# A streaming encoder step on one core: Query's streamed weight pieces split around its resident half, and two of tile 0's V groups moved from tile 2's recurrence to tile 1's top-k

## The chip, the core and the metric

The kernel runs on one core of a Trainium2 chip. The metric is device time of one execution in microseconds (us); the kernel before takes 2175.14 us (median of 3 runs, 2174.68 to 2177.02). Everything is computed in fp32.

## What is computed

One layer over a prompt (16 meta tokens and 512 tokens) and a sample of 64 tokens: RMS norm, one combined projection, forgetting attention and an HGRN2 recurrence, output projection and residual; then a retrieval of single-neuron experts (PEER). The last part is what matters here:

```python
def peer_ffn(x, w_query, sub_keys, expert_u, expert_v):     # cut
    q = (xb @ w_query).reshape(T, 8, 2, 128)                # 1024 -> 2048 columns
    s = jnp.einsum('thcd,hcnd->thcn', q, sub_keys)          # scores against 2 x 8 x 128 keys
    sa, ia = lax.top_k(s[:, :, 0], 16); sb, ib = lax.top_k(s[:, :, 1], 16)
    ...                                                     # top 16 of the 256 sums: eidx, gate
    act = jax.nn.gelu(jnp.einsum('thkd,td->thk', expert_u[eidx], xb), approximate=False)
    return jnp.einsum('thk,thkd->td', gate * act, expert_v[eidx])
```

Each token chooses 128 of 16384 rows of `expert_u` and as many of `expert_v`, each row 4 KB.

## The kernel before

The tokens are five tiles: tile 0 (sample and meta tokens) and tiles 1 to 4 of 128 prompt tokens. For each tile t the engines run attention (8 heads), the recurrence (stages named levels, masks, gram0 to gram3), norm, output projection, the second norm ("rows"), Query, and top-k. Each engine has its program in one fixed order and meets the others by semaphores alone.

**The expert rows.** GpSimd (POOL) issues 576 gathers for U (L592) and 576 for V (L598), each one row per partition, 512 KB. They land in a ring of 17 slots; a gather waits until the slot's last user is done. A U row group is multiplied by VectorE (DVE, L1387, a "dot"), a V row group by TensorE (PE, L1044) with a diagonal that ScalarE (ACT) makes from the gates (L820). Four V gathers are a quad, also called a group here; a quad is 16 matmul instructions. The gathers and their uses for tile t-1 are laid out among the stages of tile t by tables: `DOT_PLACES` for U; for V, `NEXT_PLACES` puts quads of tile t-1 at "top" of tile t itself, beside its top-k, and `LEFT_PLACES` puts what is left into tile t+1. For tile 0, which has 64 V values (16 quads) where the others have 128, the constants are `FIRST_NEXT` and `FIRST_LEFT_PLACES`. In the program's list the U gathers of tile t start only when the top-k of tile t has written its indices (`chosen`, after L1633).

**The streamed weights.** `w_out` (8 pieces) and the second half of `peer_w_query` (8 pieces) pass through five slots of `lev`, 512 KB each, and are numbered 0 to 15 in each tile. SyncE (SP) loads piece c when piece c-5 has been used:

```python
                for c in range(DC + WO_RING, 2 * DC):               # 13, 14, 15
                    sp.wait_ge(wo_used, 2 * DC * t + c - WO_RING + 1)
                    load_w_out(c)
```

Pieces 0 to 4 are asked for when the recurrence's outputs are done, 5 to 12 during the output projection, 13 to 15 as pieces 8, 9 and 10 are used. PE uses a piece in `streamed` (L1233, four matmul instructions in the profile: two halves of 512 columns, and the profile shows each matmul as two). The first half of `peer_w_query` lies resident in `arena` (L1254). Query is: wait for the turned rows, 16 resident matmuls into PSUM tensor PB, then pieces 8 to 15 into PA, then the turning of both results (L1266, which wait for ACT's copies L932 and L935), then the keys (L1275), which release DVE's top-k (L1580 on).

Of the kernel before, what the change touches and what calls it, by code (L numbers as in the profile page):

```python
# [30 lines left out]
DC = D // P  # L31
# [39 lines left out]
PARTS = TILES - 2  # L71
WO_RING = 5

LEVELS = [64, 32, 16, 8, 4, 2, 1]
NL = len(LEVELS)
NEG = -1e30
# [9 lines left out]
    ("levels", 3), ("masks", 3), ("gram1", 2), ("gram2", 2)]  # L86
NEXT_PLACES = [("top", 13)]

FIRST_NEXT = 10
FIRST_LEFT_PLACES = [("levels", 2), ("masks", 2), ("gram1", 1), ("gram2", 1)]  # L90


LATER = TILES - 1
# [21 lines left out]
def build(nc, x_prompt, x_sample, cache_kt, cache_v, cache_logf, state_hgrn, meta_tokens, w_in,  # L115
# [4 lines left out]
    with ExitStack() as ctx:  # L120
# [3 lines left out]
        def sem(name):  # L124
            return ctx.enter_context(nc.semaphore(name))

        PA, PB, PC, PD = [ctx.enter_context(nc.psum_tensor(n, [P, D], F32)) for n in ("PA", "PB", "PC", "PD")]
# [99 lines left out]
        gram_done, at_ready, ho_done, ho_evac, st_done, st_new, mix_ready = (sem(n) for n in (  # L227
            "gram_done", "at_ready", "ho_done", "ho_evac", "st_done", "st_new", "mix_ready"))
# [52 lines left out]
        def first_level(t):  # L281

            return 0 if t else 1
# [72 lines left out]
        for t in range(1, TILES):  # L356
# [6 lines left out]
            if t == 1:  # L363
                n_next = FIRST_NEXT * QUAD
            if t > 1:
                first = values_before(t - 2) + (n_next if t > 2 else FIRST_NEXT * QUAD)
                places = LEFT_PLACES if t > 2 else FIRST_LEFT_PLACES
# [8 lines left out]
            for place, quads in NEXT_PLACES:  # L376
                values_at[t, place] = range(taken, min(end, taken + (FIRST_NEXT if t == 1 else quads) * QUAD))
                taken = values_at[t, place].stop
# [582 lines left out]
        def _(pe):  # L961
# [89 lines left out]
            for t in range(TILES):  # L1051
# [175 lines left out]
                def streamed(c, out, n):  # L1227

                    slot = c % WO_RING
                    per_tile = len(range(slot, 2 * DC, WO_RING))  # L1230
                    pe.wait_ge(wo_in[slot], 16 * (per_tile * t + c // WO_RING + 1))
                    for half in range(2):
                        last = pe.matmul(out[:, half * 512:(half + 1) * 512], rows_t[:, c % DC * P:c % DC * P + n],  # L1233
                                         w_out_sb[:, slot, half * 512:(half + 1) * 512],
                                         start=(c % DC == 0), stop=(c % DC == DC - 1))
                    last.then_inc(wo_used, 1)
                    return last
# [11 lines left out]
                    pe.wait_ge(wq_in, 16 * DC)  # L1249
                nq = P if t else N_SAMPLE  # L1250
                pe.wait_ge(x1_ready, t + 1)
                for half in range(2):
                    for c in range(DC):
                        last = pe.matmul(PB[0:nq, half * 512:half * 512 + 512], rows_t[:, c * P:c * P + nq],  # L1254
                                         w_query_sb[:, c, half * 512:half * 512 + 512], start=(c == 0), stop=(c == DC - 1))
                last.then_inc(pq_done, 1)
                weighted_quads(PD, t, "pq0")
                pe.wait_ge(ho_evac, t + 1)
                for c in range(DC, 2 * DC):
                    streamed(c, PA[0:nq, :], nq)  # L1260
                weighted_quads(PD, t, "pq1")
                for n, psum in enumerate((PB, PA)):
# [26 lines left out]
        def _(eng):  # L1289
# [116 lines left out]
            for t in range(TILES):  # L1406
# [75 lines left out]
                for l in range(first_level(t), NL):  # L1482
                    m = LEVELS[l]
                    out, src = halves(lev[:, l * HW:(l + 1) * HW], HW // (2 * m), m), halves(sums, HW // (2 * m), m)
# [15 lines left out]
                for l in range(first_level(t), NL):  # L1500
                    m = LEVELS[l]
                    both = halves(lev[:, l * HW:(l + 1) * HW], HW // (2 * m), m)
# [161 lines left out]
def constant_columns():  # L1664
# [6 lines left out]
            np.where(t <= s, 0.0, NEG), np.broadcast_to(np.arange(TOPK)[None, :], (P, TOPK))]  # L1671
    for m in LEVELS:
        cols.append((s // (2 * m) == t // (2 * m)) & (s // m % 2 == 0) & (t // m % 2 == 1))
# [47 lines left out]
```

## Time and profile before

| | us |
|---|---|
| median of 3 runs | 2175.14 |
| profiled execution: its own time | 2177.34 |
| profiled execution: span of the trace | 2175.1 |
| busy PE / DVE / POOL / ACT | 1220.8 / 1263.5 / 1165.9 / 373.4 |
| moved by DMA, mean rate | 722.04 MB, 332 GB/s |

Busy time counts no waits and no issuing of DMAs by SP. A row of the chain of waits is a piece of the work that ended last: its start, its length, what it was. A row of a timeline is a run of like instructions on one engine; the bracket at its end is the idle time before it and what ended it.

### The profile page before, as it was taken

What the parts mean: (1) busy time and instruction counts of PE and PEld (TensorE: products, weight loads), DVE (VectorE), ACT (ScalarE), POOL (GpSimd) and SP (SyncE); (2) the same over time, 40 slices, a digit from 0 to 9 for tenths busy, and PEclk for the clock granted to TensorE, in tenths of its full rate; (3) what the DMA queues carried; (4) which work ended last, traced back from release to release, by engine and by line L of the source; (5) the groups of instructions that cost most, each with busy time, mean ns of one, the idle gap of its engine ahead of it and who ended that gap; (6) DMA issues with size and microseconds to landing.
All of it is one profiled execution on the core that took longest, in us unless ns stands there. A gap on an engine that the chain in (4) does not pass through costs nothing.

```text
span 2175.1 us, 15704 instructions
## 1 busy us (share of the span) xinstructions
PE 1220.8 (56%) x4932; PEld 538.3 (25%) x4932; DVE 1263.5 (58%) x2795; ACT 373.4 (17%) x1034; POOL 1165.9 (54%) x1197
## 2 busy tenths in 40 slices
PE   5898778474881365843445574445567322223564
PEld 2544343243331222311222231222332000000110
DVE  3344430877388976786564677576477566654001
ACT  1221211011030121221121121112103100002211
POOL 3012110242446774577767457776745767777673
PEclk9798879686995577976668696665778566555766
DMA  9211174485987999999999999999999999999997
GB/s 338 95 59 46 71 276 131 158 303 170 345 328 308 410 409 410 389 372 410 409 369 408 411 386 372 409 409 373 409 411 358 378 409 409 409 409 409 411 409 280
DMA packets 204307, 722.04 MB, mean 332 GB/s; under 512 B 23249, under 2 KB 25537, under 8 KB 203073
## 3 DMA queue, kind: packets, MB, share of 16 engines
q0 software_dynamic: 171168, 624.01, 73.6%
q1 hardware_dynamic: 33056, 97.03, 12.1%
q8 instruction: 40, 0.66, 0.1%
q14 instruction: 43, 0.34, 0.0%
HBM read 704.71 MB, written 15.70 MB: 331 GB/s over the span
## 4 chain that ended last, share of the span: by engine, by line
DMA 28%; PE 26%; DVE 16%; POOL 11%; issue 5%; ACT 4%; DVEq 0%; POOLq 0%; ACTq 0%
DMA arena<-peer_expert_v,idx_v 18%; POOL arena L598 7%; DMA arena<-peer_expert_u,idx_all 7%; PE PD L1044 6%; DVE arena L1387 4%; POOL arena L592 4%; PE PB L1254 4%; PE PD L966 3%; PE PB L1233 3%; DMA lev<-w_out 2%; PE PA L1233 2%; PE PA L1184 2%; DMA lev<-peer_w_query 2%; PE PB L1121 1%; PE PA L1044 1%
## 5 line engine op out<-in xcount | busy, mean ns | idle before, releaser
L592 POOL DMA_INDIRECT arena<-peer_expert_u,idx_all x576 | 543.7, 944 | 462.4 <-DVE arena L1387 185.1
L1387 DVE SCALAR_TENSOR_TENSOR arena<-arena,PC 128x1024 f32<-128x1024 f32 x576 | 677.6, 1217 | 159.6 <-DMA arena<-peer_expert_u,idx_all 152.6
L598 POOL DMA_INDIRECT arena<-peer_expert_v,idx_v x576 | 565.4, 982 | 259.7 <-issue 142.7
L1044 PE MATMUL PD<-arena,diag_v 128*32 128x512 f32 x1792 | 362.0, 883 | 516.4 <-DMA arena<-peer_expert_v,idx_v 491.2
L1044 PEld LDWEIGHTS PD<-arena,diag_v 128*32 128x32 f32 x1792 | 80.4, 141 | 755.7 <-issue 755.4
L820 ACT ACTIVATE diag_v<-consts,gate_all 128x32 f32<-128x32 f32 x576 | 137.5, 310 | 570.6 <-PE PD L1044 445.7
L966 PE MATMUL PD<-arena 128*128 128x512 f32 x384 | 178.4, 621 | 0.0
L1044 PE MATMUL PA<-arena,diag_v 128*32 128x512 f32 x512 | 96.4, 891 | 70.9 <-DMA arena<-peer_expert_v,idx_v 70.9
L1233 PE MATMUL PB<-lev,rows_t 128*128 128x512 f32 x160 | 87.9, 709 | 22.9 <-DMA lev<-w_out 17.3
L966 PEld LDWEIGHTS PD<-arena 128*128 128x128 f32 x384 | 75.1, 200 | 88.1 <-issue 87.5
L1452 DVE TENSOR_TENSOR PA<-PA,consts 128x128 f32<-128x128 f32 (+4 forms) x56 | 14.0, 250 | 140.4 <-PE PA L1102 140.1
L1121 PE MATMUL PB<-v_pr,w 128*128 128x64 f32 (+1 forms) x224 | 51.4, 374 | 59.4 <-ACT w L879 59.4
L1254 PE MATMUL PB<-arena,rows_t 128*128 128x512 f32 (+1 forms) x160 | 79.8, 663 | 5.6 <-ACT rows_t L929 5.6
L860 ACT ACTIVATE w<-PA,small 64x576 f32<-64x576 f32 (+5 forms) x48 | 25.2, 526 | 306.0 <-DVE small L1455 299.6
L1647 DVE TENSOR_TENSOR lev<-lev,PD 128x1024 f32<-128x1024 f32 x1 | 1.2, 1221 | 130.1 <-PE PA L1044 130.1
L1233 PE MATMUL PA<-lev,rows_t 128*128 128x512 f32 (+1 forms) x160 | 72.6, 600 | 4.8 <-DMA lev<-peer_w_query 4.6
L1522 DVE TENSOR_TENSOR w<-PA,level_masks 128x1024 f32<-128x1024 f32 (+1 forms) x18 | 21.8, 1209 | 80.9 <-PE PA L1185 80.9
L1121 PEld LDWEIGHTS PB<-v_pr,w 128*128 128x128 f32 (+1 forms) x224 | 43.0, 265 | 93.8 <-ACT w L879 64.3
L1102 PE MATMUL PA<-k_pr,qa 128*16 128x16 f32 (+5 forms) x96 | 38.1, 497 | 33.2 <-issue 33.2
L1044 PEld LDWEIGHTS PA<-arena,diag_v 128*32 128x32 f32 x512 | 20.0, 139 | 147.4 <-issue 147.4
L651 POOL DMA_DIRECT2D arena<-w_in x4 | 3.6, 899 | 94.6 <-PE PD L966 94.6
L1233 PEld LDWEIGHTS PB<-lev,rows_t 128*128 128x128 f32 x160 | 35.7, 231 | 73.0 <-issue 40.4
(271 smaller groups left out, 1509.7 us busy)
## 6 DMA issues: line engine op xcount, KB each, us to landing
lev<-w_out SPq DMA_DIRECT2D x40, 512.0 KB, 11.1
lev<-peer_w_query SPq DMA_DIRECT2D x40, 512.0 KB, 8.5
arena<-w_in SPq DMA_DIRECT2D x8, 2048.0 KB, 14.0
arena<-peer_expert_u,idx_all POOLq DMA_INDIRECT x576, 9.8
arena<-peer_expert_v,idx_v POOLq DMA_INDIRECT x576, 10.9
arena<-w_in POOLq DMA_DIRECT2D x4, 2048.0 KB, 8.6
act<-staged SPq DMA_DIRECT2D x4, 1796.0 KB, 8.7
staged<-arena POOLq DMA_DIRECT2D x5, 1024.0 KB, 5.2
```

Source lines behind the costliest of these rows:

```text
L592: pool.indirect_dma_start(slot, None, peer_expert_u[0], bass.IndirectOffsetOnAxis(ap=idx_all[:, k:k + 1], axis=0)).then_inc(arrived, 16)
L598: pool.indirect_dma_start(slot, None, peer_expert_v[0], bass.IndirectOffsetOnAxis(ap=idx_v[:, k:k + 1], axis=0)).then_inc(arrived, 16)
L820: return eng.activation(diag_v[:, at * STRIP:(at + 1) * STRIP], consts[:, C_FOLD:C_FOLD + STRIP], ACT.Copy, scale=gate_all[:, k:k + 1])
L860: eng.activation(w1[0:m, D * (a % 2):D * (a % 2) + n], score_psum(a, n)[0:m, :], ACT.Exp, bias=negmax[0:m, h:h + 1], accum_out=psums[0:m, ...
L966: last = pe.matmul(out, x[:, c * P:(c + 1) * P], weights[:, c, :], start=(c == 0), stop=(c == DC - 1))
L1044: ins = pe.matmul(psum[c * STRIP:(c + 1) * STRIP, half * 512:(half + 1) * 512], diag_v[:, at * STRIP:(at + 1) * STRIP], ring[slot_of[v_pla ...
L1102: last = pe.matmul(score_psum(a, n)[0:m, k0:k1], qa[:, h * P + q0:h * P + q0 + m], keys[:, h, k0:k1], start=True, stop=True)
L1121: last = pe.matmul(attended(t)[0:m, h * HD:(h + 1) * HD], w2[0:k, at:at + m], value_rows(t, q0, i, k, h // (HEADS // KV_HEADS)), start=(i ...
L1184: pe.matmul(psum[:, l * P:(l + 1) * P], both, both, start=True, stop=True)
L1233: last = pe.matmul(out[:, half * 512:(half + 1) * 512], rows_t[:, c % DC * P:c % DC * P + n], w_out_sb[:, slot, half * 512:(half + 1) * 51 ...
L1254: last = pe.matmul(PB[0:nq, half * 512:half * 512 + 512], rows_t[:, c * P:c * P + nq], w_query_sb[:, c, half * 512:half * 512 + 512], star ...
L1387: eng.scalar_tensor_tensor(out=slot, in0=slot, scalar=1.0, in1=h2_dots[:, :], op0=ALU.mult, op1=ALU.mult, accum_out=out).then_inc(free, 1)
```

## The change

The number of pieces that the ring cannot yet hold when Query starts, 3, becomes `QUERY_FIRST`. PE now uses pieces 8, 9 and 10 ahead of the resident half and pieces 11 to 15 behind it. `FIRST_NEXT` goes from 10 to 12, and the places for tile 0's remaining quads in tile 2 hold 4 instead of 6.

```diff
+QUERY_FIRST = DC - WO_RING
...
-FIRST_NEXT = 10
-FIRST_LEFT_PLACES = [("levels", 2), ("masks", 2), ("gram1", 1), ("gram2", 1)]
+FIRST_NEXT = 12
+FIRST_LEFT_PLACES = [("levels", 2), ("masks", 1), ("gram1", 1)]
...
                 pe.wait_ge(x1_ready, t + 1)
+
+                pe.wait_ge(ho_evac, t + 1)
+                for c in range(DC, DC + QUERY_FIRST):
+                    streamed(c, PA[0:nq, :], nq)
                 for half in range(2):
                     for c in range(DC):
                         last = pe.matmul(PB[0:nq, half * 512:half * 512 + 512], rows_t[:, c * P:c * P + nq],
                                          w_query_sb[:, c, half * 512:half * 512 + 512], start=(c == 0), stop=(c == DC - 1))
                 last.then_inc(pq_done, 1)
                 weighted_quads(PD, t, "pq0")
-                pe.wait_ge(ho_evac, t + 1)
-                for c in range(DC, 2 * DC):
+                for c in range(DC + QUERY_FIRST, 2 * DC):
                     streamed(c, PA[0:nq, :], nq)
```

No instruction is added or dropped on any engine. Two places, in the order in which the engines run them (line numbers of the changed file are 2 to 5 higher; a row counts matmuls, of which the profile shows two instructions each):

PE, Query of tile 1, from the turning of the rows to the keys, before and then changed.

```order
L1244 MATMUL PA<-consts,rows 128x128 x8
L1254 MATMUL PB<-arena,rows_t 128x512 x16
L1233 MATMUL PA<-lev,rows_t 128x512 x16
L1266 MATMUL PB<-consts,w 128x128 x8
L1266 MATMUL PA<-consts,w 128x128 x8
```

```order
L1246 MATMUL PA<-consts,rows 128x128 x8
L1235 MATMUL PA<-lev,rows_t 128x512 x6
L1260 MATMUL PB<-arena,rows_t 128x512 x16
L1235 MATMUL PA<-lev,rows_t 128x512 x10
L1271 MATMUL PB<-consts,w 128x128 x8
```

Six streamed matmuls (three pieces) moved ahead of the sixteen resident ones; the Querys of the other four tiles change in the same way.

POOL, from tile 0's U gathers (64) on: tile 0's V beside tile 1's top-k, then tile 2's attention and recurrence with tile 1's U, before and then changed.

```order
L592 DMA arena<-peer_expert_u,idx_all 128x1024 x64
L598 DMA arena<-peer_expert_v,idx_v 128x1024 x40
L592 DMA arena<-peer_expert_u,idx_all 128x1024 x76
L598 DMA arena<-peer_expert_v,idx_v 128x1024 x4
L592 DMA arena<-peer_expert_u,idx_all 128x1024 x2
L598 DMA arena<-peer_expert_v,idx_v 128x1024 x4
L592 DMA arena<-peer_expert_u,idx_all 128x1024 x3
L598 DMA arena<-peer_expert_v,idx_v 128x1024 x4
L592 DMA arena<-peer_expert_u,idx_all 128x1024 x2
L598 DMA arena<-peer_expert_v,idx_v 128x1024 x4
L592 DMA arena<-peer_expert_u,idx_all 128x1024 x4
L598 DMA arena<-peer_expert_v,idx_v 128x1024 x4
```

```order
L594 DMA arena<-peer_expert_u,idx_all 128x1024 x64
L600 DMA arena<-peer_expert_v,idx_v 128x1024 x48
L594 DMA arena<-peer_expert_u,idx_all 128x1024 x76
L600 DMA arena<-peer_expert_v,idx_v 128x1024 x4
L594 DMA arena<-peer_expert_u,idx_all 128x1024 x2
L600 DMA arena<-peer_expert_v,idx_v 128x1024 x4
L594 DMA arena<-peer_expert_u,idx_all 128x1024 x5
L600 DMA arena<-peer_expert_v,idx_v 128x1024 x4
L594 DMA arena<-peer_expert_u,idx_all 128x1024 x4
L600 DMA arena<-peer_expert_v,idx_v 128x1024 x4
L594 DMA arena<-peer_expert_u,idx_all 128x1024 x41
```

Eight V gathers moved from the recurrence of tile 2 to the burst beside tile 1's top-k; what stays in the recurrence is two quads at "levels", one at "masks" and one at "gram1". The second quad of "masks" and the one of "gram2" are gone there, and their 32 matmul instructions on PE with them.

## Rows read from the trace of the kernel before

**Rows 1.** The page: rate of DMA in 40 slices; the chain's shares by engine.

```profile
GB/s 338 95 59 46 71 276 131 158 303 170 345 328 308 410 409 410 389 372 410 409 369 408 411 386 372 409 409 373 409 411 358 378 409 409 409 409 409 411 409 280
...
DMA 28%; PE 26%; DVE 16%; POOL 11%; issue 5%; ACT 4%; DVEq 0%; POOLq 0%; ACTq 0%
```

**Rows 2.** The chain of waits in Query of tile 1: start, length, what.

```profile
589.26 8.55 DMA lev<-peer_w_query
```

**Rows 3.** Timeline of PE, Query of tile 1: start, length, line, count, idle before.

```profile
583.92 10.81 PE L1233 MATMUL PA<-lev,rows_t 128*128 128x512 f32 x24
595.30 1.98 PE L1233 MATMUL PA<-lev,rows_t 128*128 128x512 f32 x4 [0.58 <-DMA lev<-peer_w_query]
597.86 1.98 PE L1233 MATMUL PA<-lev,rows_t 128*128 128x512 f32 x4 [0.57 <-DMA lev<-peer_w_query]
599.68 1.04 PE L1266 MATMUL PB<-consts,w 128*128 128x128 f32 x8
```

**Rows 4.** The same timeline, Query of tile 0.

```profile
364.24 13.90 PE L1233 MATMUL PA<-lev,rows_t 128*64 128x512 f32 x32
378.06 0.71 PE L1266 MATMUL PB<-consts,w 64*128 64x64 f32 x8
```

**Rows 5.** The page's groups: Query's streamed matmuls, all tiles; busy, then idle before.

```profile
L1233 PE MATMUL PA<-lev,rows_t 128*128 128x512 f32 (+1 forms) x160 | 72.6, 600 | 4.8 <-DMA lev<-peer_w_query 4.6
```

**Rows 6.** Timeline of SP, output projection of tile 2: pieces 8 to 12 asked for.

```profile
845.57 13.95 SPq L528 DMA_DIRECT2D lev<-peer_w_query  x5
```

**Rows 7.** Timeline of POOL beside tile 1's top-k and at tile 2's start.

```profile
612.73 0.94 POOL L598 DMA_INDIRECT arena<-peer_expert_v,idx_v  x1 [13.82 <-PE PD L1044]
...
641.30 0.94 POOL L598 DMA_INDIRECT arena<-peer_expert_v,idx_v  x1 [0.31 <-PE PD L1044]
662.25 0.94 POOL L592 DMA_INDIRECT arena<-peer_expert_u,idx_all  x1 [20.01 <-DVE idx_all L1633]
```

**Rows 8.** Timeline of PE, end of tile 1's top-k and start of tile 2.

```profile
647.74 3.63 PE L1044 MATMUL PD<-arena,diag_v 128*32 128x512 f32 x16 [1.41 <-DMA arena<-peer_expert_v,idx_v]
...
664.03 2.15 PE L1102 MATMUL PA<-k_pr,qa 128*128 128x272 f32 x4 [11.23 <-issue]
```

**Rows 9.** The chain of waits, recurrence of tile 2.

```profile
785.43 9.68 DMA arena<-peer_expert_v,idx_v
```

**Rows 10.** Timeline of PE, recurrence of tile 2: both quads of "masks", then gram1.

```profile
788.25 6.19 PE L1044 MATMUL PD<-arena,diag_v 128*32 128x512 f32 x16 [1.62 <-ACT diag_v L820]
795.36 3.63 PE L1044 MATMUL PD<-arena,diag_v 128*32 128x512 f32 x16 [0.92 <-DMA arena<-peer_expert_v,idx_v]
...
804.29 3.14 PE L1184 MATMUL PA<-lev 128*128 128x128 f32 x14 [3.32 <-DVE w L1524]
```

**Rows 11.** Timeline of PE, recurrence of tile 1 (no V quads there): gram3.

```profile
522.19 1.83 PE L1184 MATMUL PA<-lev 128*128 128x128 f32 x14 [2.37 <-DVE w L1524]
```

**Rows 12.** Stretches: busy of PE, PEld, DVE, ACT, POOL; PE clock; DMA share; GB/s.

```profile
804.20:807.50 3.30, 3.21 (x17) 3.24 (x18) 2.34 (x4) 0.00 (x0) 2.49 (x3) 0.56 1.02 408
...
848.00:867.00 19.00, 8.31 (x18) 3.91 (x19) 5.81 (x12) 1.69 (x3) 0.54 (x1) 0.77 1.03 410
```

**Rows 13.** Timeline of PE, output projections of tile 2 and (last row) of tile 1.

```profile
835.64 11.61 PE L1233 MATMUL PB<-lev,rows_t 128*128 128x512 f32 x20 [1.11 <-ACT rows_t L925]
852.05 6.25 PE L1233 MATMUL PB<-lev,rows_t 128*128 128x512 f32 x10 [4.80 <-DMA lev<-w_out]
...
556.96 1.98 PE L1233 MATMUL PB<-lev,rows_t 128*128 128x512 f32 x4 [0.44 <-DMA lev<-w_out]
```

**Rows 14.** DMA queues of 848 to 862 us, output projection of tile 2: packets, MB, share.

```profile
q1 hardware_dynamic: 788, 2.88, 51.5%
q0 software_dynamic: 780, 2.85, 51.2%
```

**Rows 15.** The eight U gathers asked for at 867 to 877 us, tile 2.

```profile
DMA to landing us min/median/max: 11.9/12.0/12.1
```

**Rows 16.** Timeline of DVE, tile 2: last use of the dots of tile 1.

```profile
905.13 0.29 DVE L1404 TENSOR_TENSOR dots_all<-dots_all,gate_all 128x128 f32<-128x128 f32 x1 [10.88 <-ACT dots_all L840]
```

## The prediction, before the changed kernel was run

> **What bounds the kernel now.** I read the page first. Its 40 slices are 54.4 us each: DMA runs at 46 to 345 GB/s in the first 13 and then, from 707 us on, at 408 to 411 GB/s in most, with dips [rows 1]. The chain of waits is mixed: DMA 28%, PE 26%, DVE 16%, POOL 11% [rows 1]. So neither a busy share nor the mean rate says what an edit is worth; each stage has to be asked which wait ends last. A microsecond taken from the PE/DVE chain of a tile reaches the end if the gathers restart from that chain afterwards, which they do once per tile: the ring is full, POOL stands (13.82 us in tile 1) and the first V quads on PE, behind Query, set it going again [rows 7]. The last 450 us are one stream of gathers at the DMA limit, and start so much earlier.
>
> About 0.2% (4.3 us) is what a measurement of this kernel can tell from no change.
>
> **First part: Query's order.** In tile 1 the streamed matmuls start at 583.92 and the next work on PE at 599.68: 15.76 us for 32 instructions. In tile 0, where no wait is shown, the same 32 take 378.06 - 364.24 = 13.82 us [rows 3, 4]. The difference, 1.94 us, stands around the two shown gaps of 0.58 and 0.57 us before pieces 14 and 15, and a smaller one before 13 [rows 3]: those pieces are asked for only when 8, 9 and 10 have been used, and take 8.55 us on the chain [rows 2]. Over all tiles the gaps are 4.6 us [rows 5], four times the 1.15 of tile 1, so tiles 1 to 4 behave alike and tile 0 has nothing to win.
>
> Now 8, 9 and 10 go first. They were asked for long before: in tile 2 SP issued 8 to 12 between 845.57 and 859.52 [rows 6], all during the output projection, and between that and Query lie the sum, the second norm and the turning of the rows, some 10 us, in which PE uses no piece. Pieces 13 to 15 are then asked for some 15 us earlier, and between their request and their use lie the resident half and two pieces, over 17 us against 8.55. So the gaps go, nothing takes their place, and each of four tiles gives 1.94 us; the shown gaps alone, 1.15, are the lower price. ACT's copy of PB comes 5.2 us later than now, but 5 pieces (8.6 us) still run behind it and hide its 1 us. **4 x 1.94 = 7.8 us, bounds 4.6 and 7.8.**
>
> What is moved along: three 512 KB loads per tile now fall into the 10 us in which POOL restarts its U gathers. Those eight gathers land in 12.0 us [rows 15]; 1.5 MB more at 410 GB/s adds 3.7 us. DVE, which needs them, has 10.88 us to spare before ACT's gelu lets it go on [rows 16]. I take nothing for it.
>
> **Second part: two quads, beside tile 1's top-k.** POOL issues the last of 40 V gathers there at 641.30, at 1.25 us each, and then stands 20.01 us until the top-k has written its indices [rows 7]. Eight more are 10.0 us: they end 10 us before the U gathers of tile 2 may start, and cost POOL nothing. On PE the last quad now starts 647.74, 6.4 us after its last gather was issued; two more, 5 us apart, end at about 661.4, then the turning of tile 2's q and k (1.5 us), done near 663. PE now begins the scores at 664.03 after standing 11.23 us [rows 8]. So the cover is thin but there; if the landings took 10 us instead of 6.4, tile 2 would start up to 3 us late.
>
> What it wins is in tile 2, in two places.
>
> *Recurrence.* The chain waits there for V gathers: 9.68 us of landing before the second quad of "masks" [rows 9]. PE runs the two quads of "masks" at 788.25 and 795.36, ending at 799.0 [rows 10]. With one quad, its last gather is issued after five U and four V instead of five U and eight V: some 5 us earlier, so it lands about 790. If it ran in 3.63 us, PE would be done at 794; the first of the two took 6.19 us [rows 10], the slower kind that follows a wait, so I take 796.2. That wins 2.8 us. At "gram2" a quad of 3.63 us goes, but behind a gram without a quad PE stands 2.37 to 3.32 us for DVE's mask and sum [rows 10, 11], say 2.8, so 0.8 us is all there is. Against it stands PE's clock. After a gap of 3.32 us the 14 matmuls of gram1 took 3.14 us, at a mean granted clock of 0.56 (mostly the 1.2 GHz level); after 2.37 us in tile 1 they took 1.83 [rows 10, 11, 12]. The new gap before gram3 is some 2.8 us, between the two, so gram3 may lose 1.3 us or nothing. I take 0.5 won at gram2 and **3.3 us for the recurrence**, bounds 2 and 5.8. The Trainium skill ("TensorE: Matmul & The Clock Gate", the section "Why this matters for your kernels") says that idle gaps between bursts of matmuls send the array back to half rate, which speaks against taking a quad out. [...]
>
> *Output projection.* PE does five pieces in 11.61 us, stands 4.80 us for the sixth, and needs over 6.25 us for the last three, where twelve instructions at the 0.43 us of tile 0's Query would take 5.2: 4.8 + 1.9 = 6.7 us of waits [rows 4, 13]. It stands although POOL has been stopped: from 848 to 867 us POOL is busy 0.54 us and DMA is at 410 GB/s [rows 12]. The gathers issued before are still being served, and share the engines in halves with SP's loads: 2.85 and 2.88 MB [rows 14]. In tile 1, with no V gathers in the recurrence, the last piece waited 0.44 us [rows 13]. Take eight gathers (10.0 us of DMA) out ahead of this stage and let the chain come 3.3 us earlier, and the backlog is 6.7 us shorter: SP's loads have the engines to themselves while the ring is full. So between 0 and 6.7 us of these waits go. I take **4.5 us**, nearer to the upper end, since tile 1's row shows what a short backlog does. The two places together, 7.8 us, stay below the 10.0 us of DMA work that was moved, which is the bound of this part. The Trainium skill ("DMA: Bandwidth & Descriptors", "Queues, rings and completion order") says that each DMA engine goes round the queues that have work, which is what the halves look like. By that rule SP's loads go twice as fast from the moment at which the gathers' queue is empty, and the stage would win the whole 6.7.
>
> **Sum.** 7.8 + 3.3 + 4.5 = 15.6 us. Against the profiled execution's own time, 2177.3 (span 2175.1), that is 2161.7. The median of the runs is 2.2 us below that execution, so in terms of medians I forecast 2175.1 - 15.6, rounded: **2160 us**.
>
> **The rivals.**
>
> *A. The backlog does not shorten in time.* The twelve gathers that the "out" dots set going come in any case, right at the start of the projection, and alone can fill the queue (6.3 MB, 15 us at 410 GB/s). Then the output projection keeps its waits: 7.8 + 3.3 = 11.1 us, 2164. For it: the halves of [rows 14] are still there up to 14 us after POOL's last issue. Against it: tile 1's row.
>
> *B. The second part gives nothing.* PE's clock falls in the gaps that the quads leave (1.3 us in each of two grams), tile 2 starts a little late, the projection keeps its waits: 7.8 us, 2167.
>
> *C. The wait only changes its place.* Pieces 8 to 10 are late at the head of Query, or 11 and 12 behind it, and B holds as well: 2172 to 2175. Against it: the ten microseconds between SP's last issue and PE's first use.
>
> *D. Slower: the loads pulled forward hit the U gathers of "rows".* DVE's last dots, and so gelu, the V gates and POOL's restart, come late in tiles 1 to 4. It decides from the point where the landing of these gathers grows by more than the 10.88 us of slack [rows 16], from 12 to 23 us; to cost 20 us, enough to turn the forecast over, it must be 28. The added 1.5 MB is worth 3.7. The result would be near 2182.
>
> **How the numbers follow.** Forecast (2155 to 2162) 0.60, A 0.22, B 0.10, C 0.05, D 0.03. The likeliest is 2160. The range reaches down to the case that both parts pay their bound (7.8 + 10.0 with 1 or 2 us of luck with the clock, 2155) and up to B (2167) with a microsecond for the measurement: 2155 to 2168. All of the forecast, A and B is faster by more than 4.3 us: 0.92; C is within 0.2%: 0.05; D is slower: 0.03.
>
> **What would show it.** In the changed profile: no wait for `peer_w_query` before L1235 in any tile, and Query's 64 matmul instructions some 1.9 us shorter in tiles 1 to 4, unchanged in tile 0; POOL's idle time before tile 2's first U gather near 10 us instead of 20; 48 V gathers before it; PE's gap before tile 2's first scores near 1 us; tile 2's gram3 over 3 us earlier after its indices than now; the 4.80 us wait in tile 2's projection gone or under 2; and POOL's long wait before the "rows" gathers (L594) shorter by the projection's gain. Wrong would be: the landings of those eight U gathers above 20 us, DVE idle before L1406 near zero, tile 2's first dots late, or a gain in tile 2 that is given back as a longer wait of POOL in the top-k of tile 2 or 3.

## The result and the profile after

| | before | changed |
|---|---|---|
| median, us (5 runs each) | 2175.42 | 2164.09 |
| lowest and highest | 2174.68, 2183.06 | 2162.69, 2167.72 |
| profiled execution: its own time | 2177.34 | 2164.09 |
| profiled execution: span of the trace | 2175.1 | 2161.9 |
| busy PE / DVE / POOL / ACT | 1220.8 / 1263.5 / 1165.9 / 373.4 | 1217.1 / 1261.7 / 1169.8 / 373.4 |

The ratio of the runs is 0.9942 [0.9925, 0.9959]: 0.6% faster, 11.3 us by the medians and 13.2 us between the two profiled executions. Forecast were 2160 us and a gain of 15.6. A second set of the same kernel (below) gives 0.9939 [0.9927, 0.9952].

The page of the changed kernel: DMA rate in 40 slices, the chain's shares by engine, and the two groups of streamed matmuls (busy and mean, then idle before them).

```profile
GB/s 338 97 59 40 78 264 146 146 316 148 346 376 336 409 409 409 386 374 409 410 372 410 411 394 375 410 409 362 409 411 379 373 410 409 409 410 409 411 409 281
...
PE 27%; DMA 25%; DVE 13%; POOL 13%; issue 6%; ACT 4%; DVEq 0%; POOLq 0%; ACTq 0%
...
L1235 PE MATMUL PB<-lev,rows_t 128*128 128x512 f32 x160 | 85.1, 691 | 20.2 <-DMA lev<-w_out 14.7
...
L1235 PE MATMUL PA<-lev,rows_t 128*128 128x512 f32 (+1 forms) x160 | 81.4, 667 | 5.6 <-ACT rows_t L931 5.6
```

The 4.6 us of waiting for `peer_w_query` [rows 5] are gone; the 5.6 us in their place are the wait for the turned rows, which stood before the resident half until now (1.11 us in each tile). The DMA rate and the chain's mix hardly changed [rows 1].

**Query.** PE's timeline, Query of tile 1 (start, length, line, count, idle before):

```profile
569.39 7.84 PE L1235 MATMUL PA<-lev,rows_t 128*128 128x512 f32 x12 [1.11 <-ACT rows_t L931]
577.07 13.90 PE L1260 MATMUL PB<-arena,rows_t 128*128 128x512 f32 x32
590.81 8.75 PE L1235 MATMUL PA<-lev,rows_t 128*128 128x512 f32 x20
599.39 1.04 PE L1271 MATMUL PB<-consts,w 128*128 128x128 f32 x8
```

Nothing waits for a piece, where pieces 14 and 15 waited 0.58 and 0.57 us and their four instructions took 1.98 each [rows 3]; the last twenty now take 8.75 us. The stage from the first turning of the second norm's rows to the turning of the results takes, in tiles 1 to 4:

| us | tile 1 | 2 | 3 | 4 | sum |
|---|---|---|---|---|---|
| before | 34.13 | 34.21 | 34.85 | 34.63 | 137.8 |
| changed | 33.08 | 32.33 | 32.35 | 32.64 | 130.4 |

That is 7.4 us for the 7.8 of the sum; tile 0 kept its length (33.30, 33.53). Tile 1 won only 1.05: its first twelve instructions took 7.84 us, where twelve take 5.2 at the rate of the last twenty.

**The two quads.** POOL's timeline beside tile 1's top-k, and PE's at the end of it:

```profile
612.55 0.95 POOL L600 DMA_INDIRECT arena<-peer_expert_v,idx_v  x1 [12.66 <-PE PD L1046]
...
643.41 0.94 POOL L600 DMA_INDIRECT arena<-peer_expert_v,idx_v  x1 [0.30 <-issue]
644.66 2.48 POOL L600 DMA_INDIRECT arena<-peer_expert_v,idx_v  x1 [0.30 <-issue]
647.45 2.02 POOL L600 DMA_INDIRECT arena<-peer_expert_v,idx_v  x1 [0.30 <-issue]
...
652.27 2.14 POOL L600 DMA_INDIRECT arena<-peer_expert_v,idx_v  x1 [0.30 <-issue]
654.72 2.02 POOL L600 DMA_INDIRECT arena<-peer_expert_v,idx_v  x1 [0.30 <-issue]
662.08 0.94 POOL L594 DMA_INDIRECT arena<-peer_expert_u,idx_all  x1 [5.34 <-DVE idx_all L1638]
```

```profile
661.13 6.26 PE L1046 MATMUL PD<-arena,diag_v 128*32 128x512 f32 x16 [3.83 <-DMA arena<-peer_expert_v,idx_v]
667.32 1.06 PE L1063 MATMUL PA<-consts,act 128*64 128x128 f32 x8
```

The eight moved gathers are not eight times 1.25 us: four of them took 2.0 to 2.5. POOL waits 5.34 us for the indices, not 10, and tile 2's q and k are turned at 667.32, not 661.4 (651.29 before). The U gathers still start as before, 662.08 against 662.25 [rows 7].

**Tile 2.** Recurrence and output projection on PE:

```profile
789.99 4.98 PE L1046 MATMUL PD<-arena,diag_v 128*32 128x512 f32 x16 [3.33 <-DMA arena<-peer_expert_v,idx_v]
...
800.27 3.33 PE L1186 MATMUL PA<-lev 128*128 128x128 f32 x14 [3.31 <-DVE w L1529]
...
814.42 1.83 PE L1186 MATMUL PA<-lev 128*128 128x128 f32 x14 [2.78 <-DVE w L1529]
...
833.25 12.66 PE L1235 MATMUL PB<-lev,rows_t 128*128 128x512 f32 x24 [1.11 <-ACT rows_t L927]
846.47 1.98 PE L1235 MATMUL PB<-lev,rows_t 128*128 128x512 f32 x4 [0.56 <-DMA lev<-w_out]
849.36 1.98 PE L1235 MATMUL PB<-lev,rows_t 128*128 128x512 f32 x4 [0.90 <-DMA lev<-w_out]
```

The chain of waits there still runs through one V gather, before the quad that stayed at "masks":

```profile
780.09 9.65 DMA arena<-peer_expert_v,idx_v
```

The quad started at 789.99, where the forecast had its last landing ("about 790"), and PE is done with it at 794.90, 4.0 us earlier than with two quads. Some of that is lost at once. The clock in the stretches of gram1 and of gram3 (columns as in [rows 12]), and the quad of gram1, changed and then before:

```profile
800.20:804.80 4.60, 4.53 (x20) 4.34 (x20) 3.06 (x5) 0.00 (x0) 3.42 (x4) 0.50 1.03 408
814.40:816.50 2.10, 2.08 (x18) 2.09 (x19) 2.10 (x3) 0.00 (x0) 1.49 (x3) 1.00 1.02 406
...
804.80 4.41 PE L1046 MATMUL PD<-arena,diag_v 128*32 128x512 f32 x16
...
808.03 3.63 PE L1044 MATMUL PD<-arena,diag_v 128*32 128x512 f32 x16
```

After the gap of 3.31 us the whole of gram1 ran at a granted clock of 0.50, the 1.2 GHz level, and the quad behind it took 4.41 us instead of 3.63; after the gap of 2.78 us gram3 ran at 1.00. When the quad of gram1 is done (809.14 against 811.59), 2.5 of the 4.0 us are left.

The wait of 4.80 us in the projection [rows 13] is now 0.56 and 0.90. In tile 1's projection before, which the forecast took as the measure of a short backlog, two more pieces waited ahead of the one in [rows 13]:

```profile
551.97 1.98 PE L1233 MATMUL PB<-lev,rows_t 128*128 128x512 f32 x4 [0.50 <-DMA lev<-w_out]
554.53 1.98 PE L1233 MATMUL PB<-lev,rows_t 128*128 128x512 f32 x4 [0.58 <-DMA lev<-w_out]
```

From the first U gather to the turning of the mixed rows tile 2 takes 168.09 us (170.31 before), and from there to the turning of the second norm's rows 27.78 (33.21 before). What the two DMA queues moved at the start of the projection, before and then changed, and near its end, changed (packets, MB, share):

```profile
q0 software_dynamic: 229, 0.83, 52.4%
q1 hardware_dynamic: 228, 0.81, 50.5%
...
q1 hardware_dynamic: 248, 1.37, 86.9%
q0 software_dynamic: 60, 0.25, 15.5%
...
q1 hardware_dynamic: 221, 0.84, 52.4%
q0 software_dynamic: 222, 0.80, 50.3%
```

The first two pairs are 833 to 837 us, the third 849 to 853. The gathers' queue (q0) was all but empty when the changed projection began, so SP's loads (q1) had the engines nearly to themselves there. That lasted some 5 us, from 831 to 836: the gathers that POOL issued from 831.52 on then brought the halves back.

### The profile page after: what moved, and what is told of

It reads as the page before. It is cut to its first block, busy times and chain, and to the rows that moved or that the text cites. A ratio compares the mean times of both kernels' runs of the same rounds, so it can differ in the third digit from the quotient of the medians.

```text
span 2161.9 us, 15704 instructions
## 1 busy us (share of the span) xinstructions
PE 1217.1 (56%) x4932; PEld 542.4 (25%) x4932; DVE 1261.7 (58%) x2795; ACT 373.4 (17%) x1034; POOL 1169.8 (54%) x1197
## 4 chain that ended last, share of the span: by engine, by line
PE 27%; DMA 25%; DVE 13%; POOL 13%; issue 6%; ACT 4%; DVEq 0%; POOLq 0%; ACTq 0%
DMA arena<-peer_expert_v,idx_v 16%; POOL arena L600 9%; DMA arena<-peer_expert_u,idx_all 7%; PE PD L1046 7%; DVE arena L1392 5%; POOL arena L594 5%; PE PA L1235 4%; PE PD L968 3%; PE PB L1260 3%; PE PB L1235 3%; DMA lev<-w_out 2%; PE PB L1123 1%; PE PA L1186 1%; PE PA L1046 1%; DVE w L1529 1%
## 5 line engine op out<-in xcount | busy, mean ns | idle before, releaser
L1046 PE MATMUL PD<-arena,diag_v 128*32 128x512 f32 x1792 | 367.8, 896 | 516.1 <-DMA arena<-peer_expert_v,idx_v 491.0
L1046 PE MATMUL PA<-arena,diag_v 128*32 128x512 f32 x512 | 87.9, 821 | 79.3 <-DMA arena<-peer_expert_v,idx_v 79.3
L1235 PE MATMUL PA<-lev,rows_t 128*128 128x512 f32 (+1 forms) x160 | 81.4, 667 | 5.6 <-ACT rows_t L931 5.6
L1260 PE MATMUL PB<-arena,rows_t 128*128 128x512 f32 (+1 forms) x160 | 69.5, 592 | 0.0
L1186 PE MATMUL PA<-lev 128*128 128x128 f32 x248 | 42.6, 339 | 20.8 <-DVE w L1529 20.8
## 6 DMA issues: line engine op xcount, KB each, us to landing
arena<-peer_expert_v,idx_v POOLq DMA_INDIRECT x576, 10.5
```

Of the source, the lines that this page charges most:

```text
L1046: ins = pe.matmul(psum[c * STRIP:(c + 1) * STRIP, half * 512:(half + 1) * 512], diag_v[:, at * STRIP:(at + 1) * STRIP], ring[slot_of[v_pla ...
L1186: pe.matmul(psum[:, l * P:(l + 1) * P], both, both, start=True, stop=True)
```

## The experiments

Each is the changed kernel with the edit shown. The kernel before ran beside each of the four sets (median 2178.3, 2177.8, 2177.0 and 2177.6 us), and ratios are to it.

**1. Query's order alone.**

```diff
-FIRST_NEXT = 12
-FIRST_LEFT_PLACES = [("levels", 2), ("masks", 1), ("gram1", 1)]
+FIRST_NEXT = 10
+FIRST_LEFT_PLACES = [("levels", 2), ("masks", 2), ("gram1", 1), ("gram2", 1)]
```

> Query's pieces split as in the change (3 ahead of the resident half), tile 0's V quads left as before (10 beside tile 1's top-k). Theory (two independent gains: gaps before pieces 13 to 15; backlog of gathers in tile 2): Query is 1 to 2.3 us shorter in each of tiles 1 to 4, 4 to 8 us in all, so 2167 to 2171; the second tile's output projection keeps its waits (33.2 us from the turning of the mixed rows to the turning of the normed rows, the sixth piece waits over 4 us). Rival 1 (the pieces' new place also relieved the projection): that stretch of tile 2 falls to 28 us here too, and the time is near 2164. Rival 2 (the gain of the change was all the quads'): 2174 to 2176.

Measured: 2168.99 us, ratio 0.9956 [0.9942, 0.9971]. Query takes 33.66, 32.25, 32.30 and 32.71 us in tiles 1 to 4, 6.9 less than before; tile 2's projection keeps its 33.20. Tile 1's Query, 0.5 us shorter, stayed under the 1 us expected for each tile.

**2. The quads alone.**

```diff
-QUERY_FIRST = DC - WO_RING
+QUERY_FIRST = 0
```

> Tile 0's V quads as in the change (12 beside tile 1's top-k), Query in its old order. Theory: tile 2's recurrence is 2 to 3 us shorter and its projection stretch 28 instead of 33.2 us; Query of tiles 1 to 4 has its gaps of 0.57 us before pieces 14 and 15 again; 5 to 8 us in all, so 2167 to 2170. Rival 1 (the projection was relieved by Query's new order): 33 us in that stretch, 2172 to 2175. Rival 2 (both parts remove the same wait, so they do not add): 2164 to 2166 alone.

Measured: 2171.08 us, 0.9962 [0.9948, 0.9976], 1 us above what was expected. Tile 2's projection takes 27.96 us, the stretch from the first U gather to the mixed rows 167.57. In tile 1's Query pieces 13 to 15 wait again, 0.56 to 0.58 us each, and Query takes 139.9 us in tiles 1 to 4 (137.8 before). So both gains of tile 2, in its recurrence and in its projection, come from the quads and need nothing of Query's. The two parts, 0.44% and 0.38%, make 0.82% against 0.6% for both; with intervals of 0.15% each that may be less than the sum of both, but it isn't shown.

**3. Fourteen groups instead of twelve.**

```diff
-FIRST_NEXT = 12
-FIRST_LEFT_PLACES = [("levels", 2), ("masks", 1), ("gram1", 1)]
+FIRST_NEXT = 14
+FIRST_LEFT_PLACES = [("levels", 2)]
```

> The change, with 14 quads beside tile 1's top-k and 2 (levels) in tile 2: eight more gathers moved. Theory (the cover beside the top-k is used up on PE at 12): POOL's U gathers of tile 2 start at about 662 or up to 2 us later, PE ends the last quad at 672 or later and turns tile 2's q and k after it, so DVE's first dots of tile 2 come 5 to 10 us late; against that the recurrence gains at most 5 us and the projection at most the 1.5 us of waits that are left: 2162 to 2168, no gain. Rival (only the DMA work ahead of tile 2's projection counts): another 5 to 10 us faster, 2154 to 2159.

Measured: 2164.83 us, 0.9936 [0.9922, 0.9951], the time of the changed kernel. POOL, PE and DVE at the start of tile 2:

```profile
665.43 0.95 POOL L600 DMA_INDIRECT arena<-peer_expert_v,idx_v  x1 [0.30 <-issue]
666.69 0.95 POOL L594 DMA_INDIRECT arena<-peer_expert_u,idx_all  x1 [0.30 <-issue]
```

```profile
675.72 1.06 PE L1063 MATMUL PA<-consts,act 128*64 128x128 f32 x8
```

```profile
678.46 1.20 DVE L1392 SCALAR_TENSOR_TENSOR arena<-arena,PC 128x1024 f32<-128x1024 f32 x1
```

The cover of the burst is used up: the U gathers start 4.6 us late, q and k are turned 8.4 us later than in the changed kernel, and DVE's first dot follows them. Yet the mixed rows of tile 2 are turned at 826.78, 3.4 us before the changed kernel's 830.17: with two fewer quads in it, the tile made up for all of it. By tile 3 the lead is 0.9 us. This kernel changes two things at once, the late start and the number of quads. The kernels with the same four quads in tile 2 as the changed one separate them. In four executions (the changed kernel twice, experiment 4, the second set of experiment 6) DVE's first dot comes 7.2 to 8.1 us after the first U gather, and from that gather to the mixed rows tile 2 takes 167.9 to 168.8 us. In the seven others (2, the first set of 6, and 7 to 11 below) it comes 4.3 to 4.5 us after it, and the stretch is 167.5 to 169.2 us. The 667.32 of the changed kernel therefore cost nothing that can be seen.

**4. Six dots at the output projection instead of twelve**, so that fewer gathers are set going at its start:

```diff
-    ("out", 12), ("rows", 25)]
+    ("out", 6), ("rows", 31)]
```

> The change, with 6 of tiles 1 to 4's dots at the place 'out' (beside the output projection) instead of 12, and 31 instead of 25 at 'rows' (beside Query). Theory (SP's weight loads share the DMA engines with the gathers that the 'out' dots set going): the waits for w_out in tiles 3 and 4 (5 to 7 us each) fall by 3 to 6 us each, tile 2's rest by 1: 6 to 12 us faster than the change, 2152 to 2158; DVE's slack before the gelu falls from 9 us to about 2. Rival 1 (DMA is the limit over the whole tile, so that what the projection wins is lost when the gathers restart): 2162 to 2166, with POOL's wait beside the top-k shorter and PE's first V quads waiting for DMA. Rival 2 (DVE becomes late): slower than 2166, DVE not idle before the gelu.

Measured: 2162.83 us, 0.9926 [0.9912, 0.9941], where 2152 to 2158 was expected. The projections of tiles 3 and 4 stayed at 33.7 and 32.7 us, so what I wanted to relieve there was not relieved. Tile 1's went from 27.84 to 26.51, and its Query to 32.17. The interval overlaps the changed kernel's.

**5. The changed kernel again.**

> The changed kernel once more, unaltered, to see how far a stage of one execution can be trusted. Expected: within 0.1% of its first measurement (ratio 0.993 to 0.996). If the 2 us that went missing between the turning of Query's rows in tile 2 and the mixed rows of tile 3, and again in the next tile, belong to the change, that stretch stays near 306 us in both places; if they are the scatter of one execution, it comes out 1 us or more lower in at least one of them.

Measured: 2164.02 us. Between Query of tile 2 and the mixed rows of tile 3 the first execution took 305.9 us, this one 302.7; one tile later 306.1 and 307.9. So single stages of this length scatter by 2 to 3 us from one execution to the next. Query (131.0 us in tiles 1 to 4), tile 2's projection (27.82) and its stretch before (168.21) repeat within 0.6; tile 3's projection does not (33.76 and 35.27).

**6. One piece ahead instead of three**, run in two sets:

```diff
-QUERY_FIRST = DC - WO_RING
+QUERY_FIRST = 1
```

> The changed kernel with one piece ahead of the resident half instead of three. Theory (the wait was the ring's: piece c is asked for when c-5 has been used, lands some 8.6 us later, and only the resident half in between can cover it): piece 13 is covered, pieces 14 and 15 are not; the wait stands before piece 14 with at least 1 us in tiles 1 to 4, Query gives back 1 to 1.9 us per tile, and the time is 4 to 7 us above the changed kernel's, near that of the kernel with the quads alone (2171). Rival (any piece used ahead of the resident half gives the load enough head start, or Query gained by its order on PE and not by the loads): Query keeps its 32.3 to 33.1 us per tile, and the time is the changed kernel's.

> The kernel with one piece ahead of the resident half once more, since its first profiled execution showed Query 5.0 us longer over tiles 1 to 4 than the changed kernel's, and its five times did not show it. If the loss is real for the end, the median of this set lies 2 us or more above that of the changed kernel (2164), and both sets together too. If one piece ahead is worth as much as three, it comes to 2164 again; then the profile shows Query at 33.4 to 34.3 us again, and the time is given back in another stage.

Measured: 2164.07 us, 0.9938 [0.9925, 0.995], and 2165.56, 0.9945 [0.9932, 0.9959]. PE's timeline in Query of tile 1, first set:

```profile
587.31 10.77 PE L1235 MATMUL PA<-lev,rows_t 128*128 128x512 f32 x24
598.65 1.98 PE L1235 MATMUL PA<-lev,rows_t 128*128 128x512 f32 x4 [0.57 <-DMA lev<-peer_w_query]
```

The wait did come back, but before piece 15: piece 14 stands inside the row of 24, which takes 10.77 us instead of some 10.5. Query takes 135.4 and 136.4 us in tiles 1 to 4, 4.4 to 6.0 more than with three pieces ahead. The spans of the profiled executions follow (2165.5 and 2167.6 against 2161.9 and 2162.8), but they were the slowest of their sets both times; over all runs the mean is 2165.5 for one piece (10 runs) and 2164.7 for three (11 runs), with a scatter of 2.1 in each. So it is shown that the edit removes the ring's wait. The 4 to 7 us that were expected at the end did not come, and whether the end gets those 5 us at all stays open.

**7 and 8. What makes a gather slow.** In the changed kernel's trace the slow gathers beside the top-k end 0.8 us after a long DVE instruction does. DVE's timeline beside them:

```profile
644.04 2.29 DVE L1626 TENSOR_TENSOR w<-lev,consts 128x2048 f32<-128x2048 f32 x1
646.37 2.29 DVE L1628 TENSOR_TENSOR w<-w,lev 128x2048 f32<-128x2048 f32 x1
648.70 2.29 DVE L1629 TENSOR_REDUCE lev<-w 128x128 f32<-128x2048 f32 x1
```

The gather of 644.66 ends at 647.14, that of 647.45 at 649.47; L1626 and L1628 end at 646.33 and 648.66. In the whole trace 20 gathers start while a `tensor_tensor` of 128x2048 runs, and all 20 take 1.92 to 2.49 us; the 12 that are already under way when one starts take 0.94 to 0.95. A gather that runs beside the reduction (649.78) takes 0.94, and 0.94 is also the length beside the dots, whose second input is in PSUM. Two kernels test it. In the first the three kinds of long `tensor_tensor` (L1605, L1626, L1628) go head by head (the edit is shown for one kind, the others are alike):

```diff
-                    link(eng.tensor_tensor(same, same, idx_h[:, :, c, :].unsqueeze(2).to_broadcast(shape), ALU.mult))
+                    for h in range(ph):
+                        last = eng.tensor_tensor(same[:, h:h + 1], same[:, h:h + 1],
+                                                 idx_h[:, h:h + 1, c, :].unsqueeze(2).to_broadcast(one), ALU.mult)
+                    link(last)
```

> The changed kernel with the three kinds of long tensor_tensor in top-k (the sums of candidates, the comparison with the counting row, the product with the indices; each 128x2048 with both inputs in SBUF) done as eight of 128x256. Theory (a gather whose descriptors POOL writes while such an instruction runs has to wait until it ends): no gather over 1.5 us beside the top-k any more, where the changed kernel has 26 of 1.3 us and more; POOL issues the last V gather of tile 1's burst 4 to 5 us earlier, tile 2's q and k are turned 3 us earlier or more. DVE pays 35 more instructions per tile, 2 to 3 us, and that lies on the chain of every top-k, so the time is 5 to 12 us above the changed kernel's. Rival (what slows a gather is DVE writing 128x2048 of data, or the queue's own memory traffic, not the length of one instruction): the gathers stay at 2 us.

Measured: 2162.9 us, 0.9932 [0.992, 0.9945]. POOL at the same place, and DVE:

```profile
645.83 0.95 POOL L600 DMA_INDIRECT arena<-peer_expert_v,idx_v  x1 [0.30 <-issue]
647.08 1.04 POOL L600 DMA_INDIRECT arena<-peer_expert_v,idx_v  x1 [0.31 <-PE PD L1046]
648.42 1.16 POOL L600 DMA_INDIRECT arena<-peer_expert_v,idx_v  x1 [0.30 <-issue]
...
651.24 0.95 POOL L600 DMA_INDIRECT arena<-peer_expert_v,idx_v  x1 [0.30 <-PE PD L1046]
665.13 0.94 POOL L594 DMA_INDIRECT arena<-peer_expert_u,idx_all  x1 [12.95 <-DVE idx_all L1646]
```

```profile
645.21 2.77 DVE L1630 TENSOR_TENSOR w<-lev,consts 128x256 f32<-128x256 f32 x8
```

No gather beside a top-k is slower than 1.19 us any more. The last V gather is issued 3.5 us earlier (651.24 against 654.72) and q and k are turned at 662.88 instead of 667.32. DVE pays 0.48 us for each of the five, and the U gathers start 3.05 us later. The time was expected to rise by 5 to 12 us and didn't. Two stages show where the price went. From the turning of Query's results to the first U gather, tiles 2 to 4 take 65.2 us instead of 63.9: of DVE's 2.4 us only 1.3 arrive, since there POOL, with its slow gathers, had been the later of the two (it went from V to U gathers without a wait). And from tile 4's first U gather to the end it is 458.8 us instead of 463.8. In experiment 8 below, with more slow gathers, that stretch is 459.9, so it isn't the shorter gathers alone; what shortens it is not shown.

In the second each comparison is executed twice, with the same result:

```diff
                     link(eng.tensor_tensor(same, j.unsqueeze(3).to_broadcast(shape), iota.to_broadcast(shape),
                                            ALU.is_equal))
+                    link(eng.tensor_tensor(same, j.unsqueeze(3).to_broadcast(shape), iota.to_broadcast(shape),
+                                           ALU.is_equal))
```

> The changed kernel with each of the two comparisons in top-k executed twice (the second writes the same values again). Theory: two more instructions of 2.3 us per tile that can catch a gather: one or two more gathers over 1.9 us in each of tiles 1 to 4, and DVE's chain 4.6 us longer per tile, so the time is about 20 us above the changed kernel's. Rival (the slow gathers have their own cause, at a fixed place in POOL's sequence): their number stays at 26, at the same places in the sequence.

Measured: 2179.93 us, 1.0009 [0.9997, 1.002], 15.9 us above the changed kernel (2164.02 in the same set); about 20 was expected. The added DVE work is 4 x 2 x 2.3 = 18.4 us in tiles 1 to 4 and 2 x 1.23 = 2.5 us in tile 0, 21 us in all. In each of tiles 2 to 4 seven gathers instead of five are slow (2.0 to 2.5 us), one for each such instruction; in tile 1 it is still five, since the burst ends before the last of them. So the slow gathers follow DVE's instructions, and a microsecond on DVE in the top-k is worth about three quarters of one at the end.

**9 to 11. Halves and quarters.** Halves (128x1024) cost DVE only 0.07 us each. They were tried on the kernel of experiment 4, quarters too, and halves on the changed kernel itself:

```diff
-                    link(eng.tensor_tensor(same, same, idx_h[:, :, c, :].unsqueeze(2).to_broadcast(shape), ALU.mult))
+                    for h in range(0, ph, 4):
+                        last = eng.tensor_tensor(same[:, h:h + 4], same[:, h:h + 4],
+                                                 idx_h[:, h:h + 4, c, :].unsqueeze(2).to_broadcast(one), ALU.mult)
+                    link(last)
```

> The kernel with 6 instead of 12 dots at the output projection, and the long tensor_tensors of top-k done in two halves of 128x1024. Theory of the slow gathers: a gather waits at most for one such instruction of 1.2 us, so its worst is 2.1 us and most stay below 1.5; POOL gains 2 to 4 us beside each top-k of tiles 2 to 4, DVE pays 5 x 0.07 = 0.35 us per tile. Doing them in eight parts took away all of the 26.5 us of delay, cost DVE 2.4 us per tile and left the time as it was, so the delay is worth some 10 us in all: half of it without DVE's cost should bring 3 to 6 us, 2157 to 2160. Rival (the eighths brought nothing and cost nothing, since DVE's part and POOL's are both off the path there): 2162.8, as without the halves.

> The same kernel with those instructions done in four parts of 128x512 (0.6 us each). Theory: gathers of at most 1.5 us, as beside the 128x512 instructions of the recurrence (1.3 to 1.4); DVE pays 5 x 3 x 0.07 = 1.05 us per tile. POOL gains nearly the whole 4 to 5 us per top-k. The time is 2156 to 2160. Rival: as for the halves, 2162 to 2166.

> The changed kernel with its dots where they are and the long tensor_tensors in halves. If the halves' gain of 2 to 5 us (2157.6 against 2162.8 with 6 dots at the output projection) is that of shorter gather delays, it stands here too: 2159 to 2162 against 2164. If it needed the other places of the dots, or was the scatter of two sets, this comes to 2163 to 2165. In tile 2 the turning of q and k should come 2 to 4 us before the 667.3 of the changed kernel.

| | us, median | ratio to before | gathers over 1.25 us, their delay |
|---|---|---|---|
| changed kernel | 2164.09 | 0.9942 [0.9925, 0.9959] | 26, 26.5 us |
| halves | 2159.64 | 0.9918 [0.9898, 0.9938] | 16, 12.0 us |
| 6 dots | 2162.83 | 0.9926 [0.9912, 0.9941] | 27, 27.2 us |
| 6 dots, halves | 2157.64 | 0.9907 [0.9891, 0.9923] | 19, 13.5 us |
| 6 dots, quarters | 2159.12 | 0.9917 [0.9903, 0.993] | 9, 3.6 us |

Beside halves DVE and POOL look like this in the changed kernel with halves:

```profile
644.81 2.36 DVE L1630 TENSOR_TENSOR w<-lev,consts 128x1024 f32<-128x1024 f32 x2
647.21 2.36 DVE L1634 TENSOR_TENSOR w<-w,lev 128x1024 f32<-128x1024 f32 x2
```

```profile
645.42 1.43 POOL L600 DMA_INDIRECT arena<-peer_expert_v,idx_v  x1 [0.30 <-issue]
...
648.39 1.99 POOL L600 DMA_INDIRECT arena<-peer_expert_v,idx_v  x1 [0.30 <-issue]
663.13 0.94 POOL L594 DMA_INDIRECT arena<-peer_expert_u,idx_all  x1 [10.27 <-DVE idx_all L1646]
```

By the medians, halves go 4.5 and 5.2 us below their kernels. The intervals overlap in each pair, but both pairs moved as expected, and in tile 2 the turning of q and k comes at 664.86 instead of 667.32, within the 2 to 4 us that were expected. The traces don't show where the end gains: the profiled executions have spans of 2162.6 us with halves and 2161.9 and 2162.8 without, and with 6 dots 2161.4 with halves and 2157.2 without; with halves they were the slowest of their sets, with 6 dots alone the fastest. So the gain rests on the medians alone. The interval of 6 dots with halves lies just below both of the changed kernel's. Whether halves or quarters are better can't be told from these runs.

## Why the prediction was right, and where its sum was too large

It said faster (0.92), 2160 us, 2155 to 2168; the medians are 2164.09 and 2164.02. By its own steps:

- **Query, 7.8 us.** The mechanism was right in each point: the waits before 14 and 15 are gone, 8 to 10 were there in time, tiles 2 to 4 won 1.9 to 2.5 us. The term came to 7.4, since tile 1 won 1.05. Its Query begins on a slower TensorE: from 568 to 584 us the mean granted clock is 0.80 in the changed kernel and 0.89 before, and the first instructions are the dear ones whichever piece they use (7.84 us for twelve; before, the resident half took 15.45 instead of the 13.90 of now).
- **Recurrence, 3.3 us.** Measured 2.2 (2.1 in the second execution). The quad at "masks" came at 789.99 as forecast, and took 4.98 us, between the 3.63 and 6.19 that were weighed. Gram3, after a gap of 2.78 us, ran its 14 matmuls in 1.83 us: the slow clock there, which would have made this term 2.0, did not come true at that place. It came at gram1. The part at "masks" won more than forecast, 4.0 us for 2.8, and 1.6 of them went at gram1 and its quad, where the gap of 3.31 us was as long as before and the slow clock lasted longer (gram1's 14 took 3.33 us, 3.14 before [rows 10], and the quad 4.41 for 3.63). The forecast kept gram1 as it was. That is the term of the recurrence that was mis-sized; why the slow clock lasted longer is not shown.
- **Projection of tile 2, 4.5 us.** Measured 5.4, and in all kernels with the quads moved 5.0 to 6.1, in the one without them nothing. The short backlog, taken from tile 1's projection, was the right reading, though only one of its waits was read: the last three pieces there waited 0.50, 0.58 and 0.44 us, 1.52 in all, about what was left here too (1.46). This is what separates the forecast from rival A (the projection keeps its waits, 2164): its time is the measured one, but the waits did not stay. Half of its mechanism did happen: the gathers that the "out" dots set going came and took half of the engines again. The whole 6.7 therefore did not go: 1.46 us of waiting were left in the two rows above, and the chain of waits still passes through a landing there (8.71 us of `w_out`). The prediction applied the rule of the Trainium skill ("DMA: Bandwidth & Descriptors", "Queues, rings and completion order"), that each DMA engine goes round the queues that have work, as if the gathers' queue stayed empty. The trace agrees with the rule: with both queues at work they moved 0.84 and 0.80 MB, and with the gathers' queue all but empty SP's loads moved 1.37 MB in as long a time. The queue was empty for some 5 us only.
- **The stages sum to 15.0 us, the end got 13.2** in the profiled execution and 11 to 14 in the sets. The forecast's sum, 15.6, is 0.6 above that: Query of tile 1 and the recurrence gave less, the projection more. What is missing behind it is time that the sum has no term for. Tile 1's Query won 1.05 us, but began 0.8 us later than before (566.31 against 565.55), so POOL's first U gather of tile 2 came at 662.08 instead of 662.25; this Query begins anywhere from 565.0 to 567.8 us in the kernels whose dots are where they were. And from the turning of Query's results to the next mixed rows tiles 3 and 4 took 0.8 and 1.2 us more than before (305.9 for 305.1, 306.0 for 304.8). In the second execution these were 302.7 and 307.9, so this is no more than single stages scatter, and a cause is not shown.
- **"Cost POOL nothing", at 1.25 us each.** The price of each was wrong; that POOL's U gathers are not late held, with 5.34 us to spare instead of 10. The eight gathers moved from a stretch beside dots to one beside the top-k's long `tensor_tensor`, where four of them took 2.0 to 2.5 us. With a last quad of 6.26 us in place of 3.63 this put q and k 5.9 us behind the forecast (667.32 against 661.4). The prediction named two things for this: a price ("tile 2 would start up to 3 us late") and, as a sign of being wrong, late first dots. The sign came: DVE's first dot of tile 2 starts at 670.06 instead of 666.62. The price did not: kernels with the first dot 3 us sooner behind the first U gather take as long to the mixed rows (experiment 3).
- **Rivals.** B (the second part gives nothing) falls with the kernel of the quads alone, 0.9962 [0.9948, 0.9976]. C falls with the timeline: the page shows no wait for `peer_w_query` in Query's group any more. D needed U gathers of "rows" that take over 23 us to land; they took 13.4 (12.0 before), and DVE stood 9.00 us afterwards (10.88 before):

```profile
arena<-peer_expert_u,idx_all POOLq DMA_INDIRECT x8, 13.4
```

```profile
895.43 0.29 DVE L1409 TENSOR_TENSOR dots_all<-dots_all,gate_all 128x128 f32<-128x128 f32 x1 [9.00 <-ACT dots_all L842]
```

## What to carry to other kernels

Where a ring feeds an engine, look at what can be used before the work that needs no ring: that work then covers the next loads, at no instruction more. Move gathers not only out of the stage where they are waited for, but check what runs beside them where they go: their issue time is not a constant. And before a late start is counted as a loss, ask whether anything at the end of that stage waits for it; three numbers of one tile told that here (its first gather, its first dot, the turning of its mixed rows), read in kernels that differ in the second of them.

## What the runs showed of the hardware that was not expected

A GpSimd gather of 512 KB, 0.94 us of POOL as a rule, takes 1.9 to 2.5 us when it starts while a DVE `tensor_tensor` of 128x2048 with both inputs in SBUF is running, and ends 0.8 us after it. Beside a reduction with one input, and beside dots with one input in PSUM, it takes 0.94. A dot writes 128x1024 to SBUF in 1.2 us, as much and as long as one of the halves, and delays nothing, so it isn't the writing. Cutting the instruction into eight left at most 1.19 us, into halves at most 1.99; doubling two of them made two more gathers slow in each tile. The delay stood in the kernel before as well (22 gathers, 16 of them beside the top-k, 22.2 us in all), hidden in the mean of a group: 1001 ns for the V gathers of 900 to 1190 us is an average over 0.94 and 2.5.

The Trainium skill ("SBUF — State Buffer", "Who interferes with whom") says that a DVE instruction with two SBUF inputs contends with a GpSimd instruction that reads SBUF, and calls the port pair that they share an exclusive lock. The rows agree: a gather reads its indices from SBUF (`idx_v`, `idx_all`), the delay ends with the instruction, and it grows and shrinks with its length. In one point they differ: the same section has `tensor_tensor` as an instruction that did not stall a DMA issued from GpSimd, and here it does, so the measurement decides. Which access of the gather is held up, the reading of its indices or another, no run separates.
